# Two small tables move from before XU to behind the work buffers: 192 bytes of address for XU, the residual and T8

## The reference

```
# first block
u = rms_norm(h); z, xbc, dt, q_a, c_kv, k_rope, gates = split(u @ w_in)
h += (sigmoid(g1) * (ssd(z, xbc, dt) @ w_ssd_out) + sigmoid(g2) * (mla(q_a, c_kv) @ w_mla_out)) @ w_o
h += cross_attention(rms_norm(h), rms_norm(mem))            # w_xq, w_xkv, w_xo
h += moe(rms_norm(h))                 # 32 experts of 256 features, 2 for each token, 4 groups
h  = rms_norm(h)
# second block
u = rmsnorm(h); proj = u @ w_in_2
h += rmsnorm(concat(hgrn2(...), stick_breaking(...)) @ w_out_2)
u = rmsnorm(h); h += rmsnorm((silu(u @ gate) * (u @ up)) @ w_down_2)   # 2816 wide
h += (p @ ple_proj) * sigmoid(h @ ple_gate)
```

## Time and profile before

| | |
|---|---|
| median of 3 runs | 1048.36 us (1045.7 to 1054.06) |
| the profiled execution, span from first to last instruction | 1050.0 us |
| instructions | 19418 |
| TensorE (PE) busy | 994.2 us, 95% |
| VectorE (DVE) busy | 626.8 us, 60% |
| ScalarE (ACT) busy | 514.3 us, 49% |
| DMA, mean rate over the span | 230 GB/s |
| mean granted TensorE clock | 0.984 |

### The profile page before, as it was taken

How to read it: one execution, slowest core, us unless ns; L and a number is a source line. 1 busy time by engine, 2 the same in 40 slices (tenths; PEclk the granted TensorE clock), 3 DMA queues, 4 the chain that set the end, 5 groups by cost and what they waited for, 6 DMA issues and landing times.

```text
span 1050.0 us, 19418 instructions
## 1 busy us (share of the span) xinstructions
PE 994.2 (95%) x8568; PEld 919.7 (88%) x8568; DVE 626.8 (60%) x833; ACT 514.3 (49%) x693; POOL 19.7 (2%) x23
## 2 busy tenths in 40 slices
PE   7999999999999999999996587799999999999998
PEld 6999999899989999997673455499999999999998
DVE  6798789868766875443110110189985755555566
ACT  5576497844675563523110111277666653443453
POOL 0000021001000000000000000000000000000000
PEclk9999999999999999999998988899999999999999
DMA  7665453446245357888999999954323356555531
GB/s 290 246 236 192 170 201 124 168 156 236 81 150 212 139 224 297 315 354 333 420 420 420 421 419 423 394 192 177 139 81 128 119 206 205 196 181 189 193 121 41
DMA packets 34871, 241.74 MB, mean 230 GB/s; under 512 B 4064, under 2 KB 4448, under 8 KB 6368
## 3 DMA queue, kind: packets, MB, share of 16 engines
q1 hardware_dynamic: 33264, 233.32, 58.3%
q0 software_dynamic: 1232, 6.99, 1.9%
q10 hardware_dynamic: 288, 0.15, 0.1%
HBM read 239.36 MB, written 1.08 MB: 229 GB/s over the span
## 4 chain that ended last, share of the span: by engine, by line
PE 76%; DMA 12%; DVE 7%; ACT 2%; SPq 2%; issue 1%; DVEq 0%; ACTq 0%
PE ps L479 18%; PE ps L481 18%; PE ps L480 18%; DMA wr<-in_c_weights 8%; PE ps L568 3%; PE ps L1278 3%; DMA T8b<-in_c_weights 3%; SPq L3053 2%; DVE wlo L2044 2%; PE ps L965 1%; PE ps L1228 1%; DVE xs L2276 1%; ACT whi L1388 1%; PE ps L1305 1%; PE ps L830 1%
## 5 line engine op out<-in xcount | busy, mean ns | idle before, releaser
L2044 DVE TENSOR_TENSOR wlo<-raw,whi 128x2048 fp32r<-128x2048 f32 (+1 forms) x119 | 271.2, 2282 | 113.7 <-ACT whi L1388 113.3
L479 PE MATMUL ps<-XUh,whi 128*128 128x256 f32 x992 | 280.4, 283 | 0.7 <-DVE wlo L2044 0.6
L480 PE MATMUL ps<-XUl,whi 128*128 128x256 f32 x992 | 276.2, 278 | 0.0
L481 PE MATMUL ps<-XUh,wlo 128*128 128x256 f32 x992 | 276.2, 278 | 0.0
L1388 ACT ACTIVATE whi<-raw 128x2048 fp32r<-128x2048 f32 (+1 forms) x119 | 225.0, 1893 | 47.7 <-PE ps L481 41.2
L479 PEld LDWEIGHTS ps<-XUh,whi 128*128 128x128 f32 x992 | 186.5, 188 | 2.7 <-issue 1.7
L480 PEld LDWEIGHTS ps<-XUl,whi 128*128 128x128 f32 x992 | 188.0, 189 | 0.7 <-issue 0.5
L481 PEld LDWEIGHTS ps<-XUh,wlo 128*128 128x128 f32 x992 | 186.2, 188 | 0.0
L2976 DVE SCALAR_TENSOR_TENSOR sphs<-sphs,wsl,ps 128x256 f32<-128x256 f32 x8 | 3.8, 480 | 91.0 <-ACT sphs L2009 71.8
L479 PE MATMUL ps<-ffnah,whi 128*128 128x256 f32 x176 | 49.5, 281 | 0.0
L480 PE MATMUL ps<-ffnal,whi 128*128 128x256 f32 x176 | 49.5, 281 | 0.0
(11 more groups left out here) (624 smaller groups left out, 2372.9 us busy)
## 6 DMA issues: line engine op xcount, KB each, us to landing
raw<-in_c_weights SPq DMA_DIRECT2D x137, 1024.0 KB, 4.9
wr<-in_c_weights SPq DMA_DIRECT2D x36, 1024.0 KB, 26.1
xhi<-in_c_weights SPq DMA_DIRECT2D x12, 1024.0 KB, 26.3
xlo<-in_c_weights SPq DMA_DIRECT2D x12, 1024.0 KB, 26.5
extra<-in_c_weights SPq DMA_DIRECT2D x10, 1024.0 KB, 27.5
T<-in_c_weights SPq DMA_DIRECT2D x5, 1024.0 KB, 26.1
T8b<-in_c_weights SPq DMA_DIRECT2D x5, 1024.0 KB, 26.4
acb<-sums POOLq DMA_DIRECT2D x4, 1024.0 KB, 4.9
```

Of the source, the lines that this page charges most:

```text
L479: pe.matmul(ps, h(k), xh(k), start=start and k == 0, stop=False, skip_group_check=loose)
L480: pe.matmul(ps, h(k), xl(k), start=False, stop=False, skip_group_check=loose)
L481: t = pe.matmul(ps, l(k), xh(k), start=False, stop=stop and k == kt - 1, skip_group_check=loose)
L2044: dve.tensor_tensor(l[:, 0:n], r, h[:, 0:n].bitcast(F32), ALU.subtract).then_inc(*did("w_lo", "split", i))
```

## The change

Two tables, `lb` (128 bytes in each partition) and `flag` (16 bytes, rounded to 64), are allocated behind `T8b` instead of before `XUh`.

```diff
     hi = [sb(f"whi{i}", [128, PIECE], F32R) for i in range(3)]
     lo = [sb(f"wlo{i}", [128, PIECE], F32R) for i in range(3)]
-    lb, flag = sb("lb", [128, 32], F32), sb("flag", [128, 4], I32)
     xu_at = at[0]
     XUh, XUl = sb("XUh", [128, 8, 256], F32R), sb("XUl", [128, 8, 256], F32R)
     H = sb("H", [128, 8, 256], F32)
     t_at = at[0]
     T8, T8b = sb("T8", [128, 8, 256], F32), sb("T8b", [128, 8, 256], F32)
+    lb, flag = sb("lb", [128, 32], F32), sb("flag", [128, 4], I32)
     cst_at = at[0]
```

## The result

The changed kernel takes 1063.09 us (median of 6 runs, 1062.98 to 1064.6) and the kernel before, timed beside it, 1047.19 us (6 runs, 1045.7 to 1054.06). The ratio is 1.0153, with a 95% interval of 1.0132 to 1.0174. So 192 bytes of address cost 15.9 us. The prediction said no change and gave 1041 to 1056 us; the result lies 7 us outside. One execution among all that follow, the third of the kernel with three transposes, ran at a mean granted clock of 0.557 instead of about 0.98 and took 1665.82 us; it is left out everywhere.

What follows compares the result with a forecast made beforehand. TensorE was taken to bound the split products by matmul count times start spacing, and transfer rate the experts' stage. All five terms were 0, so the forecast was the median before, 1048.4 us, range 1041 to 1056.

Steps and rivals of the forecast that it cites:

- the split matmuls' term of the sum: 992 x 3 split-product matmuls moving XU: pace set by how a stretch is entered, not by address; taken as 0.
- a loss that none of its rows shows: An unknown effect making the kernel slower, unseen in the cited profile rows: chance 0.02.
- Rival 1: Split products: moving operands on a multiple of 128 are slow; 6.7 us more (1055.1), bound 12.2 us (1060.6); chance 0.08.
- Rival 2: Split products: the 64-byte offset makes stretches slow, so XU gets quicker; 1041.5 us, bound 1036.4; chance 0.10.
- Rival 3: Stretch entries fall otherwise in any build or run; 1041.6 if the feed-forward part turns quick, or 1051.2; chance 0.14.
- Rival 4: Rounding in `sb` leaves XU the same remainder, so nothing changes; excluded by the addresses, time as forecast, no chance given.
- Transfers: Experts' stage loads into T8 and T8b, also H and memT: no change from the receiving address, 0, within 0.3 us.
- ScalarE, VectorE: Instruction lengths on both kinds of address differ by 0.1% and 0.3%, opposite signs; taken as 0, bound 1.9 us.
- the tables: lb and flag keep their alignment, lb is touched some ten times, and no instruction moves; taken as 0.
- the plain matmuls: Line 1305, float32 weights as moving operand: median 592 ns from both kinds of address; taken as 0.
- the paces of the stretches before 800 us: Sign that the forecast is wrong: these stretches, which are entered alike, change pace together.
- The comparison of a span with the runs' times: The profiled span of 1050.0 us was put 1.6 us above the runs' median and within their reach.

Runs made afterwards that it cites:

- the kernel with three transposes: The kernel before with three short transposes instead of two in lead_in (line 487), ahead of some 15 pieces: 1047.89 us, ratio 0.9988.
- XU put back: The changed kernel with an empty 192-byte gap where the tables had been, returning XU to its old place, tables still behind: 1053.34 us, ratio 1.0068.

## Why the prediction was wrong

**The step that failed** is "Does the address set the pace? ... I take 0 for it", the split matmuls' term of the sum. Its evidence was that XUl has both paces at one address, so that the address can't matter. The first half was right and the conclusion didn't follow. That two paces occur at one address shows that something besides the address chooses between them. It doesn't show that another address would have the same two to choose from. At distance 0 neither was there: XU flowed at 120.0 ns, and its matmuls took 11.9 us more, which is the whole difference of the spans (11.7 us); all other changes nearly cancel.

**What it had not looked at.** The prediction compared each address by itself with multiples of 128. By that measure the trace held both kinds. By the measure that counts, the distance between the tile that is moved and the tile that is loaded at the same time, all moved activations stood at 192 and all moved weights at 64: the trace had never been at 0, and could not bound it. The earlier trace rows held no help, since their pairs are other tiles in another form of matmul, whose 592 ns hardly changed with the move of T (593 for T after). The prediction gave 0.02 to a loss that none of its rows shows. This was one, and with the relation of two operands never varied in the trace it deserved more.

**The size.** The prediction's own numbers give the loss once the pace is known. XUh's matmuls flow for 169.9 us at the quick pace and 180.6 us at the slow one. At 120.0 instead of 113.3 ns the first cost 10.0 us more, at 120.0 instead of 117.8 the second 3.4 us: 13.4. From the steps of even flow in the traces it is 2976 x 4.4 ns = 13.1; XU's matmuls with their pauses take 11.9 us more, since some pauses got shorter. Rival 1's bound of 1060.6 was too low, because it took 117.8 ns for the worst pace there is.

**The rivals.** Rival 1 had the sign and a time near the result, for a wrong reason: aligned moving tiles aren't slow (everything 64 up, 1.0006). Its one row, the slow swapped products, was the right row to worry about, and pointed at the distance; it got 0.08. Rival 2 fell with the same experiment. Rival 3 is real and its main term was sized well: the feed-forward part does turn between executions of one program, for 6.3 us (56 matmuls more in 168 us, 56 x 0.113), though that execution was only 2.4 us shorter in all. It moves the time within the reach of before, and didn't make this result. Rival 4 was excluded rightly.

**What was right.** Transfers, ScalarE, VectorE, the tables and the plain matmuls changed by nothing that the traces show (420 GB/s; 627.1 and 514.5 us; XU put back is quick; 592 ns). The last paragraph named the sign to look for, "the paces of the stretches before 800 us ... change together", and it is what came. The comparison of a span with the runs' times was loose: the profiled execution, at about 1052 us, lay some 3.5 us above the median that the prediction had (4.7 above that of the six runs), not 1.6.

The Trainium skill has a rule that would have spoken for "no change" here, and the runs speak against it as far as time goes. Its page "TensorE: Matmul & The Clock Gate" (section "Part 2: What happens when you issue a matmul") gives TensorE two independent read ports and says that loading the next weights takes no read bandwidth from the running matmul; the page "SBUF — State Buffer" (section "Who interferes with whom") says that TensorE never waits on anyone. By these the start of one operand relative to the other should cost nothing. Measured, it costs 1.5% of this kernel. Whether the two reads meet in the memory, or something else ties them, no run here shows.

## What to carry to other kernels

Where weight loads and matmuls alternate without a pause, here float32r matmuls of 128 x 128 by 256 columns, the byte distance between the moving and the stationary tile, modulo 256, is a parameter of the kernel: a small table put ahead of a large buffer can cost more than a percent and leave no wait in the profile. After any edit of the layout compare the distance between the starts of successive matmuls (matmuls in a window of steady flow), not busy shares or addresses by themselves, and look at whether the trace of before ever had the new relation at all. If one operand region must move, move the other by as much: everything up by 64 bytes cost nothing.

## What the runs showed of the hardware

- Float32r matmuls of 128 x 128 by 256 columns, each with its own weight load, follow each other every 113.3, 117.8 or 120.0 ns at a granted clock of 1.00. The distance of the two operands modulo 256 says which can occur: at 192 the first two, at 64 mostly the second, at 0 the third; at 128, 160 and 224 the steps are uneven, 115 to 123 ns. Where the moved tile changes within a flow, the pace changes with its distance.
- The first two paces are two rhythms of one instruction sequence. Which it takes is drawn where the flow begins, can differ between two executions of one program, and then lasts while the distance stays the same, here for up to 177.7 us.
- A mixture of distances needn't give a mixture of steps: with `whi` at 192 and `wlo` at 0 XU's three matmuls all take about 117.8 ns. With XUh at 0 and XUl at 192 the steps are uneven.
- With XU at distance 0 the time varied by 1.6 us over 6 runs, against 8.4 over 6 before. XU then has nothing to draw, but the region's tiles at 192 still have; whether this is the reason isn't shown.

Open are the mechanism, the behaviour at mixed distances, and what in an entry chooses the rhythm.
